# The expert stage of a hybrid decoder layer: inner columns in two halves instead of four quarters, paired bias products, and tails split by columns

## The reference, cut to what matters

```
def expert_rows(args):
    rows, e = args                                   # rows of one expert, width 1024
    gu = rows @ w_gate_up[e] + b_gate_up[e]          # 1024 -> 2048
    gate = jnp.minimum(gu[:, :D_FF], SWIGLU_LIMIT)
    up = jnp.clip(gu[:, D_FF:], -SWIGLU_LIMIT, SWIGLU_LIMIT)
    hid = (up + 1.0) * (gate * jax.nn.sigmoid(gate * SWIGLU_ALPHA))
    return hid @ w_down[e] + b_down[e]               # 1024 -> 1024
```

## Times and profile before

| what | value |
|---|---|
| median of 3 runs | 2520.17 us (2514.21 to 2522.26) |
| profiled execution | 2509.81 us |
| its span | 2508.1 us |
| PE busy in the span | 2352.8 us (94%) |
| DVE busy | 1879.4 us (75%) |
| ACT busy | 1470.1 us (59%) |
| moved by DMA | 629.49 MB, mean 251 GB/s |

### The profile page before, as it was taken

The page is one execution under the profiler, slowest core; times in us unless marked ns, Lnnn a source line. Parts: engine busy times, 40 slices in busy tenths (PEclk is TensorE's granted clock), DMA queues, the critical chain, the costliest instruction groups (busy, mean ns, idle before and its releaser), DMA issues.

```text
span 2508.1 us, 39656 instructions
## 1 busy us (share of the span) xinstructions
PE 2352.8 (94%) x10842; PEld 1586.2 (63%) x10843; DVE 1879.4 (75%) x2564; ACT 1470.1 (59%) x1626; POOL 238.7 (10%) x228
## 2 busy tenths in 40 slices
PE   6999999999939999999999999999999999999898
PEld 3454455545526778677777776777675676776443
DVE  4583555535467999889999998899887797998374
ACT  2113343444325787678878876687665675876244
POOL 1200000002220001000000001001010010010130
PEclk9999999999959999999999999999999999999999
DMA  6006900062327999899999999899997797997661
GB/s 195 21 13 231 345 22 22 13 208 74 103 71 260 343 369 357 306 314 370 365 354 371 368 356 322 293 367 356 316 296 255 252 364 263 367 357 248 262 215 53
DMA packets 446234, 629.49 MB, mean 251 GB/s; under 512 B 21097, under 2 KB 380521, under 8 KB 445782
## 3 DMA queue, kind: packets, MB, share of 16 engines
q1 hardware_dynamic: 391074, 532.20, 62.6%
q10 hardware_dynamic: 40304, 55.05, 6.1%
q0 software_dynamic: 14800, 41.51, 5.2%
HBM read 558.55 MB, written 68.57 MB: 250 GB/s over the span
## 4 chain that ended last, share of the span: by engine, by line
PE 77%; issue 7%; DVE 6%; DMA 4%; ACT 3%; DVEq 1%; SPq 1%; ACTq 0%; POOL 0%; POOLq 0%
PE bank L600 14%; PE bank L602 13%; PE bank L601 13%; PE bank L1326 6%; PE bank L763 4%; PE bank L1439 4%; PE bank L1349 3%; PE bank L1316 2%; PE bank L649 2%; PE bank L1369 2%; PE bank L594 2%; PE bank L1398 2%; PE bank L589 2%; PE bank L572 2%; DMA raw<-in_w_down_dram 1%
## 5 line engine op out<-in xcount | busy, mean ns | idle before, releaser
L1719 ACT ACTIVATE whi<-raw 128x2048 fp32r<-128x2048 f32 x456 | 871.5, 1917 | 377.4 <-PE bank L602 295.6
L864 DVE TENSOR_TENSOR wlo<-raw,whi 128x2048 fp32r<-128x2048 f32 x456 | 1035.8, 2283 | 49.7 <-PE bank L602 39.8
L600 PE MATMUL bank<-whi,xhi 128*128 128x512 f32 x1216 | 479.2, 394 | 0.0
L601 PE MATMUL bank<-whi,xlo 128*128 128x512 f32 x1216 | 475.4, 391 | 0.0
L602 PE MATMUL bank<-wlo,xhi 128*128 128x512 f32 x1216 | 475.3, 391 | 0.0
L600 PEld LDWEIGHTS bank<-whi,xhi 128*128 128x128 f32 x1216 | 229.0, 188 | 64.0 <-issue 19.8
L602 PEld LDWEIGHTS bank<-wlo,xhi 128*128 128x128 f32 x1216 | 228.8, 188 | 49.0
L601 PEld LDWEIGHTS bank<-whi,xlo 128*128 128x128 f32 x1216 | 228.9, 188 | 48.1
L600 PE MATMUL bank<-whi,hhi 128*128 128x512 f32 x608 | 243.2, 400 | 0.0
L601 PE MATMUL bank<-whi,hlo 128*128 128x512 f32 x608 | 237.8, 391 | 0.0
L602 PE MATMUL bank<-wlo,hhi 128*128 128x512 f32 x608 | 237.4, 390 | 0.0
(11 more groups left out here) (294 smaller groups left out, 3071.9 us busy)
## 6 DMA issues: line engine op xcount, KB each, us to landing
raw<-in_w_gate_up_dram SPq DMA_DIRECT2D x608, 512.0 KB, 5.5
raw<-in_w_down_dram SPq DMA_DIRECT2D x152, 1024.0 KB, 8.8
expert_rows<-zeros ACTq DMA_DIRECT2D x1, 33280.0 KB, 105.2
expert_rows<-ysb ACTq DMA_DIRECT2D x38, 512.0 KB, 7.1
xall<-in_x_dram SPq DMA_DIRECT2D x8, 512.0 KB, 10.4
uT<-in_w_out_dram SPq DMA_DIRECT2D x1, 4096.0 KB, 13.1
raw<-in_w_ple_gate_dram SPq DMA_DIRECT2D x1, 4096.0 KB, 19.5
h<-h_scratch SPq DMA_DIRECT2D x8, 512.0 KB, 4.9
```

The lines of the kernel that those rows point to most:

```text
L600: pe.matmul(dst, stat_hi[:, kt], hi, start=False, stop=False)
L601: pe.matmul(dst, stat_lo[:, kt], hi, start=False, stop=False)
L864: dve.tensor_tensor(wlo[:, c % LO], raw[:, c % RAW], whi[:, c % HI].bitcast(F32), ALU.subtract).then_inc(lo_ready, 1)
L1719: act.activation(whi[:, c % HI], raw[:, c % RAW], ACT.Copy).then_inc(hi_ready, 1)
```

## The change

The inner columns are done in two halves of 512. Piece c < 8 now holds 256 contraction rows (two blocks) by 512 gate and 512 up columns, so a half takes four pieces, its gate columns fill one bank and its up columns the next, and a run in memory is 2 KB. Half 0 uses banks 2 and 3, half 1 banks 0 and 1, and the down product banks 2 and 3. The elementwise operations are 512 wide and there are two rounds of them; `turn_hidden` has four transposes and comes after pieces 5 and 8; the next item's rows are turned at c = 8. A new signal `gate_done` comes when the gate bank of a half is full. On DVE clamp, wait for the sigmoid and both products stand in one block (`gate_part`, `up_part`) at c = 3 and c = 7. The bias products of two banks stand next to each other, on 2 rows each of two different 32-row tiles of the array (`bias_pair`). In a tail the four side-by-side products take four different blocks of 128 columns and the same rows, so `tail_sum` is gone; two transposes of 128 x 128 replace eight small ones. POOL gathers the rows of item 0 before `stage3_end`; ACT and DVE split the first pieces there too, and DVE makes the gate weights and row numbers for stage 5 after it.

```diff
             if c < 8:
-                j, half = c // 2, c % 2
-                rows = w_gate_up[0, bass.ds(e, 1), half * 512:half * 512 + 512, :].rearrange(
+                half, p = c // 4, c % 4
+                rows = w_gate_up[0, bass.ds(e, 1), p * 256:p * 256 + 256, :].rearrange(
                     "e (k p) n -> p (e k) n", p=P)
-                sp.dma_start(dst[:, :, 0:256], rows[:, :, j * 256:j * 256 + 256]).then_inc(raw_in[slot], 16)
-                sp.dma_start(dst[:, :, 256:512],
-                             rows[:, :, DFF + j * 256:DFF + j * 256 + 256]).then_inc(raw_in[slot], 16)
+                parts = dst.rearrange("p (k g) n -> p g k n", g=2)
+                for g in range(2):
+                    sp.dma_start(parts[:, g], rows[:, :, g * DFF + half * 512:g * DFF + half * 512 + 512]
+                                 ).then_inc(raw_in[slot], 16)
...
-        def gate_bank(q):
-            return banks(2 + q % 2)
+        def gate_base(half):
+            return 0 if half else 2
...
-                pe.wait_ge(hlo_ready, 4 * n + j)
-                for h in range(2):
-                    mm = pe.transpose(banks(HT)[:, h * P:h * P + P], hid[:, j % 2, h * P:h * P + P], ident)
+                pe.wait_ge(hid_ready, 2 * n + j + 1)
+                pe.wait_ge(hlo_ready, 2 * n + j)
+                for k in range(4):
+                    mm = pe.transpose(banks(HT)[:, k * P:k * P + P], hid[:, k * P:k * P + P], ident)
                 mm.then_inc(ht_done, 1)
 
-            def bias_row(dst, q, n):
-                mm = pe.matmul(dst, one_r[:], bsp[:, q * 512:q * 512 + 512], start=True, stop=False)
-                if q in (3, 5):
-                    mm.then_inc(bias_used[q // 5], 1)
...
+            def bias_pair(base, block, started):
+                for d in range(2):
+                    r = slice(TAIL * d, TAIL * d + 2)
+                    mm = pe.matmul(banks(base + d), one_r[r, :], bsp[r, block, :], start=not (started and d == 0),
+                                   stop=False)
+                return mm
...
-                dst = gate_bank(q)
-                if half == 0:
-                    if q == 0:
-                        pe.wait_ge(xlo_ready, n + 1)
-                        pe.wait_ge(bias_in[0], 16 * n + 16)
-                    pe.wait_ge(gu_used, 4 * n + max(q - 1, 0))
-                    bias_row(dst, q, n)
-                for j in range(4):
-                    mm = three(dst, xhi, xlo, half * 4 + j, c, j, half == 1 and j == 3)
+                half, p = c // 4, c % 4
+                base = gate_base(half)
+                if c == 0:
+                    pe.wait_ge(xlo_ready, n + 1)
+                    pe.wait_ge(y_used[0], n)
+                if c == 4:
+                    pe.wait_ge(gu_used, 2 * n)
+                for g in range(2):
+                    if p == 0 and g == 1:
+                        if half == 0:
+                            pe.wait_ge(bias_in[0], 32 * n + 32)
+                            pe.wait_ge(y_used[1], n)
+                        mm = bias_pair(base, half, True)
+                        if half == 1:
+                            mm.then_inc(bias_used[0], 1)
+                    for k in range(2):
+                        mm = three(banks(base + g), xhi, xlo, 2 * p + k, c, 2 * k + g,
+                                   p == 0 and g == 0 and k == 0, p == 3 and k == 1)
+                    if p == 3 and g == 0:
+                        mm.then_inc(gate_done, 1)
                 return mm
 
             def down_piece(n, c):
                 r = c - 8
-                pe.wait_ge(hlo_ready, 4 * n + r + 1)
+                pe.wait_ge(hlo_ready, 2 * n + r // 2 + 1)
                 if r == 0:
-                    pe.wait_ge(bias_in[1], 16 * n + 16)
+                    pe.wait_ge(bias_in[1], 32 * n + 32)
+                    pe.wait_ge(gu_used, 2 * n + 1)
+                    bias_pair(2, 2, False).then_inc(bias_used[1], 1)
                 for d in range(2):
-                    dst = banks(d)
-                    if r == 0:
-                        pe.wait_ge(y_used[d], n)
-                        bias_row(dst, 4 + d, n)
-                    if r == 1 and d == 1:
-                        turn_hidden(n, 3)
                     for kk in range(2):
-                        mm = three(dst, hhi, hlo, 2 * r + kk, c, 2 * kk + d, r == 3 and kk == 1)
+                        mm = three(banks(2 + d), hhi, hlo, 2 * r + kk, c, 2 * kk + d, False, r == 3 and kk == 1)
                     if r == 3 and d == 0:
                         mm.then_inc(y_done, 1)
...
-                    half = c % 2
-                    for j in range(GROUPS):
-                        mm = pe.matmul(banks(ACC)[j * TAIL:j * TAIL + TAIL, :], xt[:, half * 4 + j], raw[:, c % RAW, j],
-                                       start=(half == 0), stop=(half == 1))
+                    half, p = c // 4, c % 4
+                    piece = raw[:, c % RAW].rearrange("p (k g) n -> p k g n", g=2)
+                    for k in range(2):
+                        for j in range(GROUPS):
+                            mm = pe.matmul(banks(SUM if half else ACC)[j * TAIL:j * TAIL + TAIL, 0:256]
+                                           .rearrange("m (g n) -> m g n", g=2), xt[:, 2 * p + k],
+                                           piece[:, k, :, j * P:j * P + P],
+                                           start=(p == 0 and k == 0), stop=(p == 3 and k == 1))
...
-            def tail_sum(n, k1, j):
-                pe.wait_ge(sums_ready, 4 * k1 + j + 1)
-                pe.wait_ge(xlo_ready, n + 1)
-                pe.wait_ge(hid_t_ready, 4 * k1 + j)
-                pe.matmul(banks(SUM)[0:TAIL, :], sel[:], sums[:], start=True, stop=True).then_inc(u_done, 1)
...
+            def turn_tail_hidden(k1, half):
+                hold(pe, hid_t_ready, 2 * k1 + half + 1)
+                hold(pe, ht_ready, 2 * k1 + half)
+                pe.transpose(banks(XT)[:, 0:P], hid_t[:], ident).then_inc(htt_done, 1)
+            turn_rows(0)
+            pe.transpose(banks(7)[:, 0:P], ident, ident).then_inc(stage3_end, 1)
+            pe.wait_ge(stage3_end, 4)
+            pe.wait_ge(tab_in, 16)
+            pe.wait_ge(bias_zero, 1)
+            items = Items(pe, "pe", (LIVE, TWO), True)
...
-                    if c in (3, 5, 7):
-                        turn_hidden(n, (c - 3) // 2)
-                    if tail and c in (0, 2, 4, 6):
-                        turn_tail_hidden(k1, c // 2)
-                    if tail and c in (0, 2, 4):
-                        tail_sum(n, k1, c // 2 + 1)
+                    if c in (5, 8):
+                        turn_hidden(n, c // 8)
+                    if tail and c == 1:
+                        turn_tail_hidden(k1, 0)
                     if tail and c + AHEAD < PIECES:
                         tail_piece(n, k1, c + AHEAD)
+                    if tail and c == 5:
+                        turn_tail_hidden(k1, 1)
...
+            def gate_part(n, half):
+                dve.wait_ge(gate_done, 2 * n + half + 1)
+                dve.wait_ge(hid_ready, 2 * n + half)
+                dve.tensor_scalar(gat[:], banks(gate_base(half)), LIMIT, None, ALU.min).then_inc(gat_ready, 1)
+                dve.wait_ge(sig_done, 2 * n + half + 1)
                 dve.tensor_tensor(sig[:], gat[:], sig[:], ALU.mult).then_inc(gs_done, 1)
-                dve.wait_ge(gs_done, 4 * n + j + 1)
-                dve.wait_ge(ht_done, 4 * n + max(j - 1, 0))
-                dve.scalar_tensor_tensor(out=hid[:, j % 2], in0=upc[:], scalar=1.0, in1=sig[:],
+            def up_part(n, half):
+                dve.tensor_scalar(upc[:], banks(gate_base(half) + 1), LIMIT, -LIMIT, ALU.min, ALU.max).then_inc(gu_used, 1)
+                dve.wait_ge(gs_done, 2 * n + half + 1)
+                dve.wait_ge(gu_used, 2 * n + half + 1)
+                dve.wait_ge(ht_done, 2 * n + half)
+                dve.scalar_tensor_tensor(out=hid[:], in0=upc[:], scalar=1.0, in1=sig[:],
                                          op0=ALU.add, op1=ALU.mult).then_inc(hid_ready, 1)
...
+                if half == 0:
+                    dve.wait_ge(bias_t_in, 64 * fetched)
+                dve.wait_ge(tail_free, PIECES * k1 + 4 * half + 4)
+                dve.wait_ge(hid_t_ready, 2 * k1 + half)
+                dve.tensor_tensor(sums[:].rearrange("p (g n) -> p g n", g=2),
+                                  banks(SUM if half else ACC)[:, 0:256].rearrange("p (g n) -> p g n", g=2),
+                                  bias_t[:, :, half], ALU.add).then_inc(sums_ready, 1)
+                dve.wait_ge(sums_ready, 2 * k1 + half + 1)
+                dve.tensor_scalar(gat_t[:], sums[:, 0:P], LIMIT, None, ALU.min).then_inc(gat_t_ready, 1)
+                dve.tensor_scalar(upc_t[:], sums[:, P:2 * P], LIMIT, -LIMIT, ALU.min, ALU.max).then_inc(upc_t_ready, 1)
+            def tail_gated(k1, half):
...
+            for s in range(2):
```

(39 more changed lines are left out.)

351 lines of the change are left out of this document (157 added, 194 removed).

## The result

The changed kernel takes 2577.85 us (median of 4 runs, 2574.06 to 2584.47) against 2517.19 us for the kernel before (4 runs): a ratio of 1.0245, 95% interval 1.0226 to 1.0263. It is slower by 61 us; the forecast was 2486 us, faster by 34. The profiled executions agree: spans of 2572.4 and 2508.1 us.

A forecast was written before the change was run, and what follows sets the result against it. PE bounds the plain item, DVE and DMA close behind; after the change DVE's serial block makes PE wait. Plain items +16, tails -38, start -12 sum to -34 us: 2520 to 2486 us, own range 2470 to 2502, wider 2435 to 2522.

The forecast's parts named there:

- The packets' rate: Gate and up pieces: 2 KB packets move at 375 GB/s instead of 354, so 1.3 us an item go; DMA share below 1.
- Late pieces: Plain item: the 0.90 us wait for a late piece should go; no late piece was counted in DVE's block.
- DVE's wait for this sigmoid: Plain item, first half: DVE stands idle 0.66 us for the sigmoid, and the table load in front adds 0.31.
- DVE's serial block: Clamps, sigmoid and products of a half, 3.30 us, are late next: plain items 38.1 us, +16 us in all.
- Rival B: First sigmoid late behind piece 8's split, every microsecond going into DVE's chain; 1.7 us late gives 2537 us; chance 0.12.
- The bias pair: Two bias products on 32-row tiles take 0.50 us, from 0.23 if free side by side, against 0.45 before.
- The second turn: Plain item: PE waits 1.05 us for DVE's hidden tile before the second turn of inner rows.
- The wait for hlo: Plain item: PE waits another 0.5 us before the third down piece, as DVE has hlo behind two further splits.
- PE alone: Plain item if PE waits for nothing: products, bias pairs and turns sum to 36.6 us, 0.9 less than now.
- The tails: Items with a tail: 54.4 us against 59.1, so -4.7 each and -38 us for 8; bounds -45 and -22.
- the first tail sigmoid's wait: Tail item: the first sigmoid stands behind two table loads and a split, so PE waits 1.8 us.
- The start: Start of the stage: item 0's fetch starts at once, first product near 736; -12 us, bounds -15 and -4.

The follow-up runs named there:

- e4_three: Changed kernel with first sigmoid ahead of piece 8's split, sigmoid table loaded at the start of items without a tail, and tiles shifted 32 bytes: 2517.15 us.
- e2_sigma: Changed kernel with one ScalarE move: the first half's sigmoid ahead of the high split of piece 8 instead of behind it; 2520.47 us.
- e11_between: Changed kernel with, on VectorE, the low split of piece 7 between the first half's lower clamp and its gated product; 2526.16 us.
- e3_table: Changed kernel with a one-column sigmoid on ScalarE at the start of items without a tail, so the table is loaded there; 2544.08 us.
- e10_hidden: Against e7_rows, VectorE does the second half's hlo ahead of the low split of the next item's piece 0 instead of behind it; 2497.56 us.
- e7_rows: Against e4_three, the two bias products of a block run over all 128 rows instead of 2 rows each; 2511.81 us.
- e8_keep: Changed kernel plus 8 unused products of 512 columns on PE ahead of the second turn of inner rows; 2588.44 us.
- e13_low: Against e4_three, xhi and xlo placed lower in SBUF, at bytes 167456 and 171552 of a partition; 2514.93 us.

## Why the prediction was wrong

*The packets' rate:* right. Gate and up pieces were taken at 375 GB/s in 2 KB packets; e4_three shows 376, the DMA share is below 1, and the packets are worth 26 us in the repaired kernel.

*Late pieces:* the step that failed. The prediction says of the 0.90 us wait for a piece that it "should go", and its block on DVE has no late piece in it: ACT's split of piece 8 starts at T + 0.29. T is at the end of PE's work on piece 2 (the 13 steps that the prediction counts lead one step past the start of the last product). In the item shown T is 1305.99 and the split starts at 1309.05, T + 3.06. Of the 2.8 us more, 1.6 are piece 7, which had landed late too (ACT was at it until 1307.90), and 1.2 are piece 8, which took 12.0 us to land. Behind it stand the table load and the first sigmoid. The prediction gave DVE's wait for this sigmoid 0.66 us and 0.31 for the table load; measured, it is 3.1 in the mean of eleven items. The 2.1 us more go one to one into the item (see the table above): 38.1 + 2.1 = 40.2 of the 41.3. That DVE's serial block decides was right, and it is the very chain that the prediction added up. A late piece in it was put at nothing on the strength of a faster rate; in the trace ACT waited 48.5 us for down pieces in all and 47.7 for gate and up pieces, against 23.3 and 24.7 before. The rest, 1.1 us an item, is not taken apart by any run; the lower clock is about 0.3 of it.

*Rival B* named this mechanism with its place and got too small a chance, 0.12. Its rule, that every microsecond goes straight into DVE's chain, is what e2_sigma, e11_between and e3_table show; its example was a landing of 10.2 us and 1.7 us late. With the landing that was measured, 0.14 + 11.3 - 8.9 = 2.5 us late, it gives 30 x 2.5 = 75 us over 2486, thus 2561: the nearest of the recorded cases, and 17 us short. What it has against itself, that longer packets would shorten the landing, came out the other way.

*The bias pair:* taken at 0.50 us, the upper row; measured 1.10 less two steps of 0.23, 0.64. The sign was right, the size above the upper bound: the prediction's row did not have the slower step behind the pair. The Trainium skill's rule in TensorEngine Tiling (Array Packing), Key Properties, "Mode switching requires drain", fits: the way into the pair takes 0.33 instead of 0.23 us, and the step behind the first full product after it 0.34.

*The second turn:* forecast 1.05 us, measured 2.0; in e4_three, with the sigmoid on time, 0.2 us. *The wait for hlo:* forecast 0.5 in every item, measured 0.54 to 0.62 in five of eleven; in e4_three 0.5 in ten of eleven, and e10_hidden shows that it was removable.

*PE alone:* forecast 36.6 us an item, measured 424.0 / 11 = 38.5. Missing were the longer step (0.6 us), the pairs (0.4), the lower clock in half of the items (0.7: PE is busy 37.9 us an item in e2_sigma, at a clock of 1.00), and 0.1 us at several piece starts. Little of it is on the path (e7_rows, e8_keep, e13_low).

*The tails:* 54.4 forecast, 53.3 measured in the same way; the first tail sigmoid's wait 1.8 and 1.89. *The start:* 12 us forecast, 7.2 measured. Had plain items taken the 38.1 us of the forecast, 30 x 3.2 = 96 us would be gone and the time 2482, near the 2486 that were forecast: the tails (8 us more) and the start (5 us less) nearly cancel, which is luck, and the plain item was wrong.

## What to carry to other kernels

Where an in-order engine waits for another's answer with a queue of work behind it that others need, a microsecond of that wait can come back in every item, however idle the engine is on average: put other work between what it sends off and what it waits for. Find out which wait it is; here some 172 us of idle time of the same engine, before other work, stayed as they were while the kernel gained 57. When a block is made coarser, follow what is queued behind its wait on each engine, what lands before what, and which other transfers now share that landing. A stalled tensor engine at a lower clock may be only the sign of such a queue; fill the stall with dummy work before blaming it.

## What was not expected of the hardware

- After PE had stood still some 2 us, the granted clock was 0.50 for about 3.4 us in some items and stayed 1.00 in others; with filler work in the same place it stayed at 1.00 in all eleven plain items looked at.
- The step of fp32r products was 0.233 or 0.227 us depending on where the standing operand lies in SBUF, in one kernel and not in another.
- At the start of an item the gather of the next rows and, behind it, the rows' output share the queues with the weights: between 1299 and 1301 us, in the gather, the weights' queue moved 0.26 MB in 2 us at 73.5% of the engines' time, a third of its usual rate.
